# Distance-bias rows of a two-block transformer kernel: made on all 128 partitions by PE products between the projection's tiles, and stored from there

## The reference, cut to what matters

```python
def _t5_bucket(dist):
    exact = RPB_BUCKETS // 2
    d = jnp.maximum(dist, 0)
    df = jnp.maximum(d, 1).astype(jnp.float32)
    large = exact + (jnp.log(df / exact) / math.log(RPB_MAX_DIST / exact)
                     * (RPB_BUCKETS - exact)).astype(jnp.int32)
    large = jnp.minimum(large, RPB_BUCKETS - 1)
    return jnp.where(d < exact, d, large)
...
    bias = jnp.transpose(bias_tab[_t5_bucket(rdist * dilation)], (2, 0, 1))
...
    s = jnp.einsum('bnqhd,bnkhd->bnhqk', qb, kb).astype(jnp.float32) * dh ** -0.5 + bias
```

## Time and profile before

| | us |
|---|---|
| median of 3 runs | 3767.77 (3765.06 to 3768.7) |
| the profiled execution, its time | 3771.5 |
| the profiled execution, its span | 3769.7 |
| PE busy in the span | 3068.9 |
| DVE busy | 1734.7 |
| POOL busy | 1521.4 |
| ACT busy | 645.7 |
| mean granted TensorE clock, share of full speed | 0.871 |

### The profile page before, as it was taken

How to read it: one execution, slowest core, us unless ns; L and a number is a source line. 1 busy time by engine, 2 the same in 40 slices (tenths; PEclk the granted TensorE clock), 3 DMA queues, 4 the chain that set the end, 5 groups by cost and what they waited for, 6 DMA issues and landing times. The chain is left out here.

```text
span 3769.7 us, 33430 instructions
## 1 busy us (share of the span) xinstructions
PE 3068.9 (81%) x12858; PEld 2268.9 (60%) x12858; DVE 1734.7 (46%) x2065; ACT 645.7 (17%) x1005; POOL 1521.4 (40%) x430
## 2 busy tenths in 40 slices
PE   6633935889978999678578998999794689989999
PEld 5432524768756666447236876887573258858877
DVE  2007445544336666432365335881213464337840
ACT  0001220010024555321231001000103130010000
POOL 5230000047611111135005765776462027747766
PEclk9865557989988999778679998999896799989999
DMA  3970000012226888412011221222221202212223
GB/s 133 61 74 15 25 1 0 1 67 100 79 113 255 319 312 321 187 63 78 27 27 58 100 90 65 92 90 89 87 89 49 27 23 91 100 67 86 94 90 112
DMA packets 77110, 353.79 MB, mean 94 GB/s; under 512 B 30900, under 2 KB 31284, under 8 KB 38358
## 3 DMA queue, kind: packets, MB, share of 16 engines
q1 hardware_dynamic: 62824, 333.03, 24.7%
q10 hardware_dynamic: 2886, 10.10, 4.1%
q0 software_dynamic: 11232, 8.43, 0.7%
HBM read 353.19 MB, written 30.80 MB: 102 GB/s over the span
## 5 line engine op out<-in xcount | busy, mean ns | idle before, releaser
L129 POOL TENSOR_TENSOR w_hi<-w_raw,w_zero 128x2048 fp32r<-128x2048 f32 x174 | 627.7, 3607 | 1798.4 <-PE bank L156 1641.9
L156 PE MATMUL bank<-xh,w_hi 128*128 128x512 f32 x1864 | 754.2, 405 | 146.5 <-POOL w_lo L132 53.1
L132 POOL TENSOR_TENSOR w_lo<-w_raw,w_hi 128x2048 fp32r<-128x2048 f32 x174 | 812.8, 4671 | 13.6
L157 PE MATMUL bank<-xl,w_hi 128*128 128x512 f32 x1864 | 749.6, 402 | 0.0
L158 PE MATMUL bank<-xh,w_lo 128*128 128x512 f32 x1864 | 747.9, 401 | 0.0
L156 PEld LDWEIGHTS bank<-xh,w_hi 128*128 128x128 f32 x1864 | 357.1, 192 | 253.9 <-issue 98.3
L158 PEld LDWEIGHTS bank<-xh,w_lo 128*128 128x128 f32 x1864 | 357.8, 192 | 88.4
L157 PEld LDWEIGHTS bank<-xl,w_hi 128*128 128x128 f32 x1864 | 358.4, 192 | 85.1
L499 DVE TENSOR_TENSOR part<-sig,bank 128x512 f32<-128x512 f32 x96 | 66.1, 689 | 382.1 <-PE bank L158 381.7
L2119 DVE TENSOR_TENSOR fl<-work,fh 128x512 fp32r<-128x512 f32 x44 | 211.2, 4801 | 1.5
L536 DVE SCALAR_TENSOR_TENSOR res<-res,bank 128x512 f32<-128x512 f32 x40 | 27.5, 688 | 375.7 <-PE bank L158 375.7
(11 more groups left out here) (497 smaller groups left out, 4820.0 us busy)
## 6 DMA issues: line engine op xcount, KB each, us to landing
w_raw<-weights SPq DMA_DIRECT2D x216, 1024.0 KB, 4.8
raw<-weights SPq DMA_DIRECT2D x51, 1024.0 KB, 8.9
res<-weights SPq DMA_DIRECT2D x26, 1024.0 KB, 6.2
distance_bias<-bias_rows ACTq DMA_DIRECT2D x8, 512.0 KB, 72.9
na_bias<-grid_bias SPq DMA_DIRECT2D x16, 240.0 KB, 7.0
strips<-distance_bias SPq DMA_DIRECT2D x8, 448.0 KB, 3.1
raw<-picked_rows SPq DMA_DIRECT2D x6, 512.0 KB, 6.5
tabs<-tables SPq DMA_DIRECT2D x2, 1408.0 KB, 6.3
```

What stands on the lines that cost most here:

```text
L129: pool.tensor_tensor(self.hi[:, s, :], self.raw[:, s, :], self.zero[:, 0:1].to_broadcast([128, CHUNK]), ALU.add).then_inc(self.rounded, 1)
L132: pool.tensor_tensor(self.lo[:, s, :], self.raw[:, s, :], self.hi[:, s, :].bitcast(F32), ALU.subtract).then_inc(self.split, 1)
L156: self.released(pe.matmul(out, hi, moving[0], start=start, stop=False))
L157: pe.matmul(out, hi, moving[1], start=False, stop=False)
```

## The change

The projection's PE list makes the distance products head by head, one head behind each of the tiles 6 to 13. The weights of such a product are one column of the table read 128 times over (`tab[0:34, h:h + 1].to_broadcast([34, 128])`), so the result of 128 x 512 has the head's row on every partition. ACT, no longer DVE, copies the two banks into one of two buffers (`bias_rows` is now 2 x 1024) and issues the head's store, 128 partitions of 4 KB. It waits for the store two heads back before it writes a buffer again, and PE waits for the copy of the head before.

```diff
@@ -288,6 +288,8 @@
                 last.then_inc(product_ready, 1)
                 if j == tiles // 2 and "tensor" in aside_run:
                     aside_run["tensor"](pe, *aside_sems)
+                if 6 <= j < 14 and "tensor_heads" in aside_run:
+                    aside_run["tensor_heads"](pe, *aside_sems, heads=[j - 6])
...
-    def scalar(act, rows_in, bias_ready, bias_copied, bias_stored):
-        act.wait_ge(bias_copied, 2)
+    def scalar(act, rows_in, bias_ready, bias_copied, bias_even, bias_odd):
+        stored = (bias_even, bias_odd)
         for h in range(8):
-            row = out[h:h + 1, :].rearrange("p (a x) -> p a x", a=1).to_broadcast([1, 128, 1024])
-            act.dma_start(bias_dram[h:h + 1, :, :], row).then_inc(bias_stored, 16)
-        act.wait_ge(bias_stored, 128)
-
-    def tensor(pe, rows_in, bias_ready, bias_copied, bias_stored):
-        pe.wait_ge(rows_in, 32)
-        for j in range(2):
-            pe.matmul(k.bank[2 + j][0:8, :], tab[0:34, :], rows[0:34, 512 * j:512 * j + 512], start=True,
-                      stop=True).then_inc(bias_ready, 1)
-
-    def vector(dve, rows_in, bias_ready, bias_copied, bias_stored):
-        for j in range(2):
-            dve.wait_ge(bias_ready, j + 1)
-            dve.tensor_copy(out[0:8, 512 * j:512 * j + 512], k.bank[2 + j][0:8, :]).then_inc(bias_copied, 1)
-    return names, dict(loads=loads, scalar=scalar, tensor=tensor, vector=vector)
+            for j in range(2):
+                act.wait_ge(bias_ready, 2 * h + j + 1)
+                if h >= 2 and j == 0:
+                    act.wait_ge(stored[h % 2], 16 * (h // 2))
+                act.activation(out[:, h % 2, 512 * j:512 * j + 512], k.bank[2 + j][:, :], ACT.Copy).then_inc(
+                    bias_copied, 1)
+            act.wait_ge(bias_copied, 2 * h + 2)
+            act.dma_start(bias_dram[h, :, :], out[:, h % 2, :]).then_inc(stored[h % 2], 16)
+        for s in stored:
+            act.wait_ge(s, 64)
+
+    def tensor(pe, rows_in, bias_ready, bias_copied, bias_even, bias_odd, heads):
+        if 0 in heads:
+            pe.wait_ge(rows_in, 32)
+        for h in heads:
+            for j in range(2):
+                if h:
+                    pe.wait_ge(bias_copied, 2 * h - 1 + j)
+                pe.matmul(k.bank[2 + j][:, :], tab[0:34, h:h + 1].to_broadcast([34, 128]),
+                          rows[0:34, 512 * j:512 * j + 512], start=True, stop=True).then_inc(bias_ready, 1)
+    return names, dict(loads=loads, scalar=scalar, tensor_heads=tensor)
...
-                with memory(k, rows=(1024,), tab=(8,), bias_rows=(1024,)) as (rows, tab, bias_rows):
+                with memory(k, rows=(1024,), tab=(8,), bias_rows=(2, 1024)) as (rows, tab, bias_rows):
```

More of the change, by code:

```diff
@@ L659, in distance_bias @@
 def distance_bias(k, bias_dram, rows, tab, out):
-    names = ("rows_in", "bias_ready", "bias_copied", "bias_stored")
+    names = ("rows_in", "bias_ready", "bias_copied", "bias_even", "bias_odd")
     def loads(sp, rows_in, *_):
```

## The result

The changed kernel took 3683.14 us at the median of 4 runs (3676.43 to 3685.34), the kernel before beside it 3766.41 (3764.28 to 3768.7): 83.3 us less, a ratio of 0.9776 with a 95% interval of 0.9759 to 0.9793. The profiled execution took 3676.43 us, its span is 3674.6.

What follows compares the result with a forecast made beforehand. Slow bias-row stores starving weight loads in the first projection were taken as the bound. Terms of 45.7, 31.7 and 1.3 us made 78.7 us less, from 3767.8 to 3689.1 us, range 3684 to 3700.

Steps and rivals of the forecast that it cites:

- term 1: First projection up to tile 20's copy: no weight starvation, eight product pairs at 2.01 us each added, 45.7 us less.
- The experts' rows: MoE stage: full-width f32 weight loads of 0.19 us follow at 0.43 us, so wider weights load covered.
- Rival (a): Projection products: weight loads exposed, adding 6.1 us, total 3695.2 us; chance 5%.
- The stores: Eight 512 KB distance-bias stores from 128 partitions in the projection: 2.6 us each, no waits.
- Rival (c): Bias stores no faster, held by target or ACT queue at 19.3 us each, total 3780.6 us; chance 3%.
- (b): Projection: stores still hold weight loads up, in proportion, leaving 11.1 us of PE waits, total 3700.2 us; chance 7%.
- (d): Projection: weight loads are late by themselves, waits stay and hide the new products, no change; chance 3%.
- term 2: Projection's token-major products, tile 20's copy to SP's last load: 59.5 us becomes 27.8, 31.7 us less.
- The later layer's rows: One layer's identical pair of 256-column products: 11.36 us to the first copy, 13.20 to the second, 24.56 in all.
- term 3: Start of the next stage: activation table already loaded during the projection, 1.3 us less.
- the barrier passes the gain on: All-engine barrier ending the projection stage: its gain reaches the total, nothing later gives it back except a new wait.
- the low end of the range: 3684 us, from execution scatter of 3765.06 to 3768.7 and some 2 us for a clock staying high into the next stage.

Runs made afterwards that it cites:

- the form with two products in all: Kernel before, with the table widened to 34 x 128, two 128 x 512 products and stores from 16 partitions a head: 3667.59 us, ratio 0.975.
- the run with one partition: The changed kernel, but each store again reads partition 0 alone, 128 times over: 3753.61 us, ratio 0.9984.
- the pair of runs that differ in it: Sixteen partitions a head, made from the kernel before, with the two banks copied by DVE (3667.59 us) or by ACT (3667.92 us).
- the five variants: Products behind tiles 12 to 19, one-partition stores, and sixteen partitions a head adjacent, interleaved or ACT-copied: 3678.68, 3753.61, 3667.59, 3668.03, 3667.92 us.
- late form: The changed kernel with its eight pairs of products behind tiles 12 to 19 instead of 6 to 13: 3678.68 us, ratio 0.9779.
- the section on the kernel before: The kernel before, profiled a second time with no edit, on another chip: 3760.96 us.

## Why the prediction was right, and where it failed

**The products (term 1).** Forecast 45.7 us, measured 212.34 - 167.32 = 45.0. A head's two products cost 7.70 - 5.60 = 2.10 us, not 2.01. The widened weights were covered but for 0.09 us a head, which is 0.7 us over eight. It comes with the width and not with the new waits: the form with two products in all has the same 7.70 us between the copies at 94.97 and 102.67, where before had 7.61. The experts' rows were the right ones to read: in the trace after, a load with 0.19 us follows the one before at 0.43 us, as there. Rival (a), and with it the Trainium skill's rule of "TensorE: Matmul & The Clock Gate" (The mechanism, on packing), would have made the tiles 8.4 us apart. That holds for its one sentence on the row group; the same section also lets a load go ahead into the background weight buffer, and the spacing here agrees with that.

```profile
80.22 0.19 PEld L690 LDWEIGHTS bank<-rows,tab 34*128 34x128 f32 x1 [0.24 <-issue]
80.65 0.19 PEld L690 LDWEIGHTS bank<-rows,tab 34*128 34x128 f32 x1 [0.24 <-issue]
```

**The stores.** Forecast 2.6 us, measured 2.8 at the median, with nothing waiting for them. token_rows, a transfer of the same shape on another queue, was the right neighbour. The source was named as the cause on the strength of 27 GB/s alone; the run with one partition shows it. Rival (c) is out by the landings, (b) and (d) by the list of waits.

**The token-major products (term 2).** Forecast 27.8 us from tile 20's copy to the end of SP's last load, measured 194.94 - 167.32 = 27.6. The later layer's rows carried it: 11.36 and 13.14 us to the two copies, against 11.36 and 13.20 there. That POOL's conversion and not the copies ends the stage was right.

**The activation table (term 3).** Forecast 1.3 us, and 1.27 at the first activation in the pair of runs that differ in it. The Trainium skill's drain of some 1.38 us ("ScalarE: Activation LUTs", on what a table load costs) would have shown there as 2.7.

**The sum.** 78.7 us forecast, 78.4 measured at the strips. That the barrier passes the gain on was right too: in all profiles the strips mark the same point of the same later program.

**The step that failed** is the low end of the range, the sentence that took "the scatter between executions, 3765.06 to 3768.7 before" and some 2 us for a warmer clock behind the stage. It took the scatter of the times, and with it everything behind the stage, from three runs. The forecast lies 6.0 us above the measured 3683.14. The steps of the stage add 0.3 us to the other side (78.7 forecast, 78.4 measured); 1.4 us come from the start of the sum, 3767.8 where the kernel before took 3766.4 beside the change; and 4.9 come from behind the strips, where the sum had nothing.

Three runs showed 3.6 us of scatter; 15 runs of the same kernel on the first chip of the experiments went from 3751.08 to 3776.4, 25 us. The span behind the strips was 3410.9 and 3400.4 us in two profiles of before, 3394.2 and 3399.9 in two of the change, and 3389.7 to 3404.6 in the five variants. The median of three from which the sum started lay 5.5 us above that of the 15 (3767.77 - 3762.3), and the medians of the changed kernel and of its late form, which cost the same, are 4.5 us apart (3683.14, 3681.7, 3678.68). The two together, as independent, are some 7 us, an estimate, and with that the range would have reached down to 3682.

Started from the better median, the steps hold: 3762.3 - 78.4 = 3683.9 with what they measured, within 2.2 us of both medians of the changed kernel. All three medians named lie below 3684, so a part of the 4.9 us may be a lasting gain of a few us behind the stage; as the section on the kernel before says, that stays open.

The other 2 us of that sentence, for a clock that stays high into the next stage, are shown by no run and did not come: that stage's first two passes keep PE busy 2.07 us in the trace after, from 197.14, as in the trace before, from 275.25, both at a granted clock of 0.50, which is 1.2 GHz.

## What to carry to other kernels

Stores that read one partition over and over ran at 27 GB/s here and kept the DMA engines 96% busy while they did, and the weight loads beside them came late; look for such a transfer, and make the row on many partitions first. Sixteen source partitions were enough here, and they cost two matmuls where 128 had cost sixteen. Before a range is written in a kernel with many lightly loaded stages, count how often its times were taken: a spread seen over three runs says little of the next one.

## What the runs showed of the hardware

- Eight stores of 512 KB: 19.3 us each from one partition, 3.8 to 4.0 from 16 adjacent ones, 3.1 from 16 that lie 8 apart, 2.8 to landing from all 128. All of them with weight loads beside them.
- With stores from one partition, DMA engines read 96% busy at 60 GB/s. The busy share alone does not tell that a transfer makes progress.
- Stores from one partition, two in flight and PE paced by them, with 14.1 us more of products: 3753.6 us. The same stores all queued at once, without these products: 3762.3. In the first form POOL waited 24.4 us for weights, in the second 110.8. The forecast for the first, rival (c), was 3780.6.
- A float32 product of 34 x 128 weights and 512 columns costs 1.05 us by the spacing of the tiles, and 1.00 with 8 columns of weights (2.10 and 2.01 us for two, at a granted clock of 1.00).
- The same 76 matmuls of one light stage took PE 38.0 or 43.8 us of busy time in two executions of one program, at a mean granted clock of 0.77 and 0.67 of full speed.
